# Gated linear attention, a block's output: all 128-row products first, then the 64-row products alternating between the halves of the rows

## The reference

```
qe = q*exp(bcum); ke = k*exp(-bcum); kd = k*exp(b_last - bcum)
A = where(causal, qe @ ke.T, 0)          # within a chunk
o_intra = A @ v
for each chunk c:  o_inter[c] = qe[c] @ S;  S = decay[c]*S + kd[c].T @ v[c]
o = o_intra + o_inter
```

## Time and profile before

| | |
|---|---|
| Median of 3 runs | 2107.91 us |
| Lowest and highest | 2107.56 and 2107.99 us |
| Span of the profiled execution | 2105.4 us |
| Time of that execution beside its span | none given apart from the span |
| Busy: TensorE, VectorE, ScalarE, GpSimd | 98%, 58%, 37%, 18% |
| Mean granted TensorE clock | 0.991 of full speed |

### The profile page before, as it was taken

The page is one execution under the profiler, slowest core; times in us unless marked ns, Lnnn a source line. Parts: engine busy times, 40 slices in busy tenths (PEclk is TensorE's granted clock), DMA queues, the critical chain, the costliest instruction groups (busy, mean ns, idle before and its releaser), DMA issues.

```text
span 2105.4 us, 38895 instructions
## 1 busy us (share of the span) xinstructions
PE 2055.8 (98%) x16516; PEld 1996.7 (95%) x16516; DVE 1225.6 (58%) x1667; ACT 787.3 (37%) x1209; POOL 379.8 (18%) x238
## 2 busy tenths in 40 slices
PE   6999999999999999999989999999999999999998
PEld 6999889998999999999989989899989999999998
DVE  4897667754555454354539875687445565433445
ACT  4313533543543332233233144336435433422332
POOL 0694000311103000000308930002111030000003
PEclk9999999999999999999999999999999999999999
DMA  7524413222222222222445242222223222222223
GB/s 234 96 88 77 81 61 111 81 74 94 108 101 81 100 92 89 100 80 77 138 120 92 83 63 79 90 82 81 93 81 121 81 101 84 91 90 95 100 75 125
DMA packets 70038, 199.54 MB, mean 95 GB/s; under 512 B 41554, under 2 KB 42706, under 8 KB 51408
## 3 DMA queue, kind: packets, MB, share of 16 engines
q1 hardware_dynamic: 26144, 177.50, 25.4%
q10 hardware_dynamic: 43760, 20.11, 5.4%
HBM read 187.42 MB, written 12.29 MB: 95 GB/s over the span
## 4 chain that ended last, share of the span: by engine, by line
PE 43%; DVE 5%; issue 1%; ACT 1%; POOL 0%; DVEq 0%; POOLq 0%
PE acc L604 40%; DVE cacc L1258 1%; DVE wlo L1264 1%; PE m L698 1%; PE m L687 1%; DVE q L1255 1%; PE m L781 0%; ACT tmp L942 0%; DVE sct L1258 0%; PE m L711 0%; PE m L773 0%; PE m L618 0%; DVE gt L1255 0%; PE m L808 0%; PE m L818 0%
## 5 line engine op out<-in xcount | busy, mean ns | idle before, releaser
L604 PE MATMUL acc<-xhi,wlo 128*128 128x260 f32 x3680 | 755.5, 287 | 29.0 <-PEq L567 19.6
L604 PE MATMUL acc<-xhi,whi 128*128 128x260 f32 x3680 | 744.4, 284 | 0.0
L604 PE MATMUL acc<-xlo,whi 128*128 128x260 f32 x3680 | 743.5, 284 | 0.0
L604 PEld LDWEIGHTS acc<-xhi,wlo 128*128 128x128 f32 x3680 | 572.6, 190 | 47.0 <-issue 40.6
L604 PEld LDWEIGHTS acc<-xhi,whi 128*128 128x128 f32 x3680 | 570.3, 189 | 0.0
L604 PEld LDWEIGHTS acc<-xlo,whi 128*128 128x128 f32 x3680 | 570.0, 190 | 0.0
L1264 DVE TENSOR_TENSOR wlo<-raw,whi 128x1024 fp32r<-128x1024 f32 (+3 forms) x344 | 433.4, 1268 | 37.3 <-ACT whi L959 35.9
L959 ACT ACTIVATE whi<-raw 128x1024 fp32r<-128x1024 f32 (+3 forms) x344 | 332.0, 994 | 259.1 <-PE acc L604 198.2
L942 ACT ACTIVATE gt<-gt 128x520 f32<-128x520 f32 x226 | 144.3, 638 | 218.8 <-DVE gt L1255 213.9
L1255 DVE TENSOR_TENSOR gt<-acc,rstd 128x520 f32<-128x520 f32 x80 | 55.9, 698 | 218.1 <-PE acc L604 194.0
L604 PE MATMUL acc<-hhi,whi 128*128 128x260 f32 x704 | 141.5, 282 | 0.0
(11 more groups left out here) (224 smaller groups left out, 2167.2 us busy)
## 6 DMA issues: line engine op xcount, KB each, us to landing
raw<-in_wt SPq DMA_DIRECT2D x142, 1024.0 KB, 4.9
raw<-in_wt SPq DMA_DIRECT2D x16, 768.0 KB, 4.3
raw<-in_wt SPq DMA_DIRECT2D x16, 640.0 KB, 3.8
x<-yt ACTq DMA_DIRECT2D x2, 2080.0 KB, 9.5
yt<-x ACTq DMA_DIRECT2D x16, 260.0 KB, 2.1
x<-in_xt SPq DMA_DIRECT2D x4, 520.0 KB, 5.2
yt<-in_xt SPq DMA_DIRECT2D x1, 2080.0 KB, 16.2
s<-in_gs ACTq DMA_DIRECT2D x4, 512.0 KB, 3.5
```

The costliest lines, as they stand in the source:

```text
L604: ins = nc.tensor.matmul(out[:, h], a, b[:, h * TH:h * TH + TH], start=first and n == 0, stop=last and n == 2)
```

## The change

The four products over 128 rows come first, then all products over 64 rows. Those are issued for p, then for the chunk cc, then for hh, so that neighbours lie in different halves of the rows and write to different banks. The first product in each bank (p = 0) alone has `start`; the one for p = 1 goes to the same bank without it. Nothing else is changed, and the number of matmuls is the same.

```diff
@@ -767,19 +767,24 @@
                                 pe.wait_ge(s["ga_m"], b + 1)
                                 if b:
                                     pe.wait_ge(s["ga_out"], b)
-                                for h in range(4):
-                                    p, hh = h // 2, h % 2
-                                    r = slice(hh * HEAD, hh * HEAD + HEAD)
-                                    nc.tensor.matmul(m4[:, 2 + hh, p * P:p * P + P], vtok[:, b, h * P:h * P + P],
-                                                     am[:, 2 * hh + p], start=True, stop=False)
+                                for p in range(2):
+                                    for hh in range(2):
+                                        h = 2 * p + hh
+                                        nc.tensor.matmul(m4[:, 2 + hh, p * P:p * P + P], vtok[:, b, h * P:h * P + P],
+                                                         am[:, 2 * hh + p], start=p == 0, stop=False,
+                                                         skip_group_check=True)
+                                for p in range(2):
                                     for cc in range(2):
                                         ch = 2 * b + cc
                                         if ch == 0:
                                             continue
                                         t0 = ch * CHUNK
                                         o = p * P + cc * CHUNK
-                                        ins = nc.tensor.matmul(m4[:, 2 + hh, o:o + CHUNK], sh[r, ch - 1, p],
-                                                               gq[r, p, t0:t0 + CHUNK], start=False, stop=cc == 1)
+                                        for hh in range(2):
+                                            r = slice(hh * HEAD, hh * HEAD + HEAD)
+                                            ins = nc.tensor.matmul(m4[:, 2 + hh, o:o + CHUNK], sh[r, ch - 1, p],
+                                                                   gq[r, p, t0:t0 + CHUNK], start=False, stop=cc == 1,
+                                                                   skip_group_check=True)
                                 ins.then_inc(s["ga_o"], 1)
                         for b in range(NBLK):
                             if n == G_A[b]:
```

## The result

The changed kernel takes 2088.2 us (median of 4 runs, 2087.9 to 2090.7) against 2107.7 us before (4 runs). The ratio is 0.9921, with an interval of 0.9909 to 0.9933: faster by 14 to 19 us. Two further groups of runs put the change at medians of 2087.2 and 2088.7 us.

The account below looks back on a forecast made before the run. TensorE's own time was taken to bound the kernel. The steps' 14.4 us and the clock's 0.7 made 15.1 us less than 2107.9, 2092.8, said as 2093.0 us, with a range of 2089.5 to 2099.8.

Parts of the forecast that it names:

- That TensorE's time is the kernel's time: Whole kernel: TensorE is busy 98% of the span, so a microsecond taken out of it comes off the end.
- The sum of the steps: Changed steps, both layers: 2.00 us against 3.91, block 0 1.56 against 3.02; 14.4 us saved in all.
- twins: 64-row passes in different row halves start in pairs, 0.11 us for two, as at L793; about 6.2 us saved.
- the serial part of the prediction: Changed steps: three of four returns to 128 rows removed in each of 8 steps, about 8.2 us saved.
- Rival (a): At L781 twins do not form; steps 2.88 us (block 0: 2.00), saving 8.2 us, 2099.7 us; chance 0.07.
- (b): Behind the steps, half or more of the saving goes into waits at L604; 2101 to 2108 us; chance 0.05.
- (c): At the steps every change of half empties the array, 0.20 us each; saves 0.8 a layer, 2106.3 us; chance 0.03.
- (d): At the steps each change of half also exposes the weight load, 0.40 us; 8 us slower, 2115.9 us; chance 0.01.
- (e): Clock falls behind many more steps, 1.4 us each; ten more undo the gain; no chance of its own beyond the range.
- The clock: Behind layer 1's last step: falls to granted clock 0.50 cost 1.4 us; half a fall less, -0.7 us.

Follow-up runs that it names:

- e3: The change with each p finished before the next, adding one return to 128 rows in each step; median 2092.0 us, ratio to before 0.9928.
- e1: The change without alternation: all 64-row products of one half of the rows, then all of the other; median 2092.3 us, ratio to before 0.9924.
- e7: The change with each 64-row product made three times; 2101.3 us, ratio to before 0.9972.
- e6: The kernel before with each block's step split: heads 0 and 1 behind one slot, 2 and 3 behind the next; 2102.6 us, ratio 0.9981.
- e9: The change with 64-row products made twice, one half before the other; 2106.2 us, ratio to before 1.0000. Its rival: falls came from changing between 128 and 64 rows.
- e8: The kernel before, unchanged, run again for a second profile; mean 2107.5 us, ratio to before 1.0005.

## Why the prediction was right, and where it was short

**That TensorE's time is the kernel's time** held: no new wait behind the steps, and in the profiled pair as much came off the span (19.0 us) as off TensorE's busy time (19.7).

**The sum of the steps** was 2.00 and 1.56 us; measured 2.02 and 1.58. The saving worked out was 14.4 us; measured 2 x (3 x (3.91 - 2.02) + 3.02 - 1.58) = 14.2. The score step L793 was the right row to read the twins from.

**The price of a return** was 0.34 us in the expectation of e3, and is 0.34 there. The rows of the prediction give the same between single passes: 1.00 us for a head behind the first, against 6 x 0.11 for its passes. So three returns fewer in each of 8 steps are 24 x 0.34 = 8.2 us, the serial part of the prediction. The rest, 6.0 us, is twins. But the split is not the same as "without alternation": without it (e1) the steps still save 2 x (3 x (3.91 - 2.51) + 3.02 - 1.58) = 11.3 us, since half of the twins form by themselves. Rival (a) with its 2099.7 us was priced as if none did; it is refuted as to twins, and its price would have been wrong for plain serial order.

**The rivals.** (b) has no new wait behind the steps in the list of waits. (c) and (d) needed a step of 3.8 us or more. (e) did not come; the clock went the other way.

**The clock** is the term that was mis-sized. The prediction took -0.7 us, "half a fall less", with -2.8 to +2.8 as the bounds. Over all runs the clock took 17.0 us before and 14.0 with the change, 3.0 us less. With 14.2 from the steps that makes 17.2; the means differ by 18.2, and 1.0 us stays open, two standard errors of the times at full clock. The forecast would have been 2090.5 us with the right term. Another 1.4 us is its base: it was taken from a median of 2107.9, where the mean of 55 runs is 2106.5. The step of the prediction that fell short is the counting: it looked at one profile and one fall at the steps, and took half of it as saved. The kernel before has four places for a fall there, and the second profile had falls at all four. Nor does that fall stand behind the step, as the prediction has it: it begins 0.7 us before the step's end. The prediction had measured the steps of layer 0 alone and taken layer 1's to be the same; they are, but for this one.

**What makes it fall** is shown in part. It is not the length of the stretch alone (e7: as long, in twins, mean clock 0.9937) and not the number of returns alone (e6: as many, mean clock 0.9938). Long and thin together, one half of the rows at a time with returns between, is the kernel before, at 0.9919. Whether long and thin without returns is enough stays open: e9's mean clock leans that way by two standard errors.

The profiles, read place by place, say something that the means do not. At the end of a layer's last step the two profiles of the kernel before have a fall in 3 of 4 places. The ten profiles of the change and its variants (all but e6 and e8) have none in 20, e7 and e9 with their long steps among them. Behind the decode tokens' products it is 3 of 4 and 9 of 20, so falls there did not go away. The falls at the steps, 1.5 in an execution at the prediction's 1.4 us each, come to about 2.1 of the 3.0 us, an estimate from two profiles. What the kernel before has and those ten lack is three returns to 128 rows within a step (e3 has one, the others none). So the rival of e9, the changes of rows, is not excluded, and no run here has such returns in a long step of twins.

The Trainium skill says, in "TensorE: Matmul & The Clock Gate", Part 1, that the clock gate is set by how busy TensorE has been recently. The mean clocks of e6 and e7 agree with it as far as they go; e9, with one half of the rows at a time and no fall behind its steps, does not show it.

## What to carry to other kernels

Where products over 64 rows stand among products over 128 rows, gather them: each change there and back cost 0.34 us here, between single passes and between twins. The order inside the gathered group mattered less, since TensorE itself pairs passes of the two halves that lie up to about four apart: with eight passes of a half in a row 0.5 us a step was lost, against 1.0 for three returns. It matters more the longer one half stands alone. With sixteen and sixteen (e9) the step took 4.30 us, where twins would take 2.02 + 16 x 0.056 = 2.9, an estimate from e7's rate. Look in the trace for a place where the kernel already does what a change proposes; one such row (L793) gave the price to 1%. And before two profiles of a kernel with a varying clock are compared, set its mean over several runs apart from the work: of the 19.0 us between two spans here, 14.2 were the steps.

## What the runs showed of the hardware that was not expected

- Passes over different halves of the rows start together without being neighbours in the program, and so out of its order: in e6 the first pass of L796 started at 467.89 us, ahead of three passes of L783 that the program issues before it (468.04, 468.15, 468.26). With eight passes of one half ahead of eight of the other, the first of the second half began 0.006 us behind the fifth of the first. A step took 2.51 us there, 2.07 with four and four in turn, 2.02 with two and two.
- Twins kept their rate over 48 passes, 0.056 us a pass (e7).
- The same matmuls cost 4 us less of 2107 when they were spread over two places (0.9981, 0.9972 to 0.9990), with the same time at full clock. So small products can have a price that does not show in their own rows.
